# Second dense stage of a two-block kernel: first projection in two blocks around the input products, output projection in quarters, mixed rows by halves, one gate row spread last

## The reference

```python
mod = c_act @ w_ada[l] + b_ada[l]
sh1, sc1, g1, sh2, sc2, g2 = jnp.split(mod, 6, axis=-1)
h = _modulate(_rmsnorm(x, norm1_g[l]), sh1, sc1)
q, k, v, u = jnp.split(h @ w_in[l], [D_ATTN, 2 * D_ATTN, 3 * D_ATTN], axis=-1)
...
attn_out = _diff_attention(q, k, v, lam, lambda_init, subln_g[l])   # 4 heads, two softmaxes each
ssm_out = _s5(u, ...)              # diagonal state space, gelu z, then z * sigmoid(z @ w_glu + b_glu)
mix = jnp.concatenate([attn_out, ssm_out], axis=-1) @ w_out[l]
x = x + g1[:, None, :] * mix
h = _modulate(_rmsnorm(x, norm2_g[l]), sh2, sc2)
x = x + g2[:, None, :] * _moe(h, ...)       # 32 experts, top 4, w1 1024x2048, w2 1024x1024
```

## Time and profile before

| | |
|---|---|
| median of 3 runs | 1909.75 us (1908.7 to 1909.96) |
| profiled execution: its time, its span | 1911.13 us, 1909.1 us |
| PE busy | 1616.4 us (85%) |
| DVE busy | 470.0 us (25%) |
| ACT busy | 249.8 us (13%) |
| mean DMA rate over the span | 358 GB/s |
| dense stage two | 778.9 to 952.0 us of the span |
| mixture two | 952.0 to 1900 us of the span |

### The profile page before, as it was taken

One profiled execution on the slowest core, in us unless ns is written; L12 is line 12 of the kernel. 1 busy time (PEld: TensorE's weight loads), 2 busy tenths in 40 slices (PEclk: granted clock), 3 DMA queues, 4 the chain that ended last, 5 costly groups with the idle time before them and its releaser, 6 DMA issues. The chain is left out here.

```text
span 1909.1 us, 23699 instructions
## 1 busy us (share of the span) xinstructions
PE 1616.4 (85%) x9872; PEld 783.0 (41%) x9872; DVE 470.0 (25%) x749; ACT 249.8 (13%) x451; POOL 116.0 (6%) x267
## 2 busy tenths in 40 slices
PE   6999998676766667797799898989989989899896
PEld 6665545333323334464543333333333333333332
DVE  2632313110101100597421121221221212212123
ACT  2123322000000001114210000000000000000001
POOL 0030000793000000000000000000000000000000
PEclk9999998888778888897799999999999999999998
DMA  9556875999999999613568999999999999999994
GB/s 327 211 177 252 270 264 200 426 426 428 428 428 428 428 428 424 220 76 146 229 290 355 428 428 426 428 427 428 428 428 428 427 428 427 427 427 428 428 428 196
DMA packets 90270, 683.75 MB, mean 358 GB/s; under 512 B 18103, under 2 KB 21352, under 8 KB 53352
## 3 DMA queue, kind: packets, MB, share of 16 engines
q1 hardware_dynamic: 86466, 678.72, 86.3%
q10 hardware_dynamic: 3750, 4.26, 0.7%
HBM read 681.91 MB, written 1.05 MB: 358 GB/s over the span
## 5 line engine op out<-in xcount | busy, mean ns | idle before, releaser
L1391 PE MATMUL ps<-ring,hT 128*64 128x512 f32 x2048 | 464.4, 611 | 38.9 <-DMA ring<-in_w_dram 38.8
L1391 PEld LDWEIGHTS ps<-ring,hT 128*64 128x64 f32 x2048 | 158.1, 141 | 342.3 <-issue 341.4
L1386 PE MATMUL ps<-ring,hT 128*32 128x256 f32 x2048 | 161.6, 481 | 95.5 <-DMA ring<-in_w_up_dram 60.9
L1434 PE MATMUL ps<-ring,Wp 128*64 128x512 f32 x992 | 224.7, 612 | 14.3 <-ACT Wp L1476 14.3
L1386 PEld LDWEIGHTS ps<-ring,hT 128*32 128x32 f32 x2048 | 81.8, 133 | 176.4 <-issue 122.8
L1434 PEld LDWEIGHTS ps<-ring,Wp 128*64 128x64 f32 x992 | 71.7, 141 | 157.6 <-issue 139.7
L1525 DVE TENSOR_SCALAR Wp<-ps 128x1024 f32<-128x1024 f32 x16 | 19.6, 1225 | 430.0 <-PE ps L1391 430.0
L967 PE MATMUL ps<-ring,hT 128*128 128x512 f32 (+1 forms) x288 | 120.8, 573 | 0.0
L1469 ACT ACTIVATE mod<-Wp 128x1024 f32<-128x1024 f32 x16 | 17.0, 1061 | 782.5 <-DVE Wp L1525 782.5
L1430 PE MATMUL ps<-ring,m_hidT 128*32 128x512 f32 x480 | 69.2, 729 | 31.5 <-DMA ring<-in_w_down_dram 31.5
L1541 DVE TENSOR_TENSOR hT<-ps,Wp 128x512 f32<-128x512 f32 x32 | 20.6, 686 | 240.3 <-PE ps L1434 240.3
(11 more groups left out here) (453 smaller groups left out, 1435.2 us busy)
## 6 DMA issues: line engine op xcount, KB each, us to landing
ring<-in_w_dram SPq DMA_DIRECT2D x190, 2048.0 KB, 15.6
ring<-in_w_gate_dram SPq DMA_DIRECT2D x32, 2048.0 KB, 19.0
ring<-in_w_up_dram SPq DMA_DIRECT2D x32, 2048.0 KB, 20.1
ring<-in_w_down_dram SPq DMA_DIRECT2D x30, 2048.0 KB, 20.2
ring<-in_w_in_dram SPq DMA_DIRECT2D x14, 2048.0 KB, 15.6
ring<-in_w_ada_dram SPq DMA_DIRECT2D x12, 2048.0 KB, 11.4
ring<-in_w_out_dram SPq DMA_DIRECT2D x4, 2048.0 KB, 16.7
Wp<-in_w_down_dram SPq DMA_DIRECT2D x2, 2048.0 KB, 11.1
```

Of the source, the lines that this page charges most:

```text
L1386: ins = nt.matmul(ps[r:r + 32, u // 2, c:c + 256], xgT[:, t, x:x + 32], w[:, 512 * t:512 * t + 512].rearrange("q (p b s) -> q b p s", b=2, ...
L1391: ins = nt.matmul(ps[64 * e:64 * e + 64, b, :], xgT[:, 2 * u + t, 64 * e:64 * e + 64], w[:, c:c + 512], start=False, stop=u == 3 and t == ...
L1434: ins = nt.matmul(ps[r, C0 + h, :], hidT[:, 4 * u + t, r], w[:, c:c + 512], start=u == 0 and t == 0, stop=4 * u + t == FT - 1, tile_positi ...
```

## The change

`P0` keeps its first block in bank 6 and puts the second in bank 5; ACT copies each block as it is done, and `I0` is issued from inside the second block, before its fourth product. `Out` and `L` go by quarters (tile i, half h): `L0` to `L3`, of which the last two now stand behind `Glu`, and the state space half in four quarters, each with its own signal. DVE gates `ssT` in two halves, adds the mixed rows by halves, and starts the norm of tile 0 before the last half is added. ACT squares by halves, loads the sigmoid table early and the square root table ahead of its copies. `D` moves behind `H3`, `G2` ahead of `S1`. The g2 row is spread after the logits instead of between the output products.

```diff
@@ ORDER2 and the SP queue
-        ORDER2 = "P0 I0 R0 P1 I1 P2 C0 R1 P3 I2 G0 J0 P4 C1 R2 G1 H0 P5 S0 P6 C2 S1 I3 Y X0 X1 G2 E0 P7 T0 O0 E1 T1 O1 J1 J2 " \
-                 "U3 H1 H2 N M K L0 V3 C3 D G3 J3 H3 L1 Glu Out"
+        ORDER2 = "P0 R0 P1 I1 P2 C0 R1 P3 I2 G0 J0 P4 C1 R2 G1 H0 P5 S0 P6 C2 G2 S1 I3 Y X0 X1 E0 P7 T0 O0 E1 T1 O1 J1 J2 " \
+                 "U3 H1 H2 N M K L0 V3 C3 G3 J3 H3 D L1 Glu L2 L3 Out"
...
-                        sp.wait_ge(g_m, 1)
+                        sp.wait_ge(g_o, 1)
                         sp.dma_start(area[:, 1, :], moe2_src(0, AT + 1)).then_inc(aside2[1], 16)
@@ PE, P
+                                if n == 0 and cb == 1 and t == 3:
+                                    pe.wait_ge(p_ak, 1)
+                                    I(0)
-                                ins = nt.matmul(ps[:, 6 + n % 2, cb * 256:cb * 256 + 256], w[:, t, c:c + 128], hT[:, t, :],
+                                ins = nt.matmul(ps[:, 5, 0:256] if n == 0 and cb else ps[:, 6 + n % 2, cb * 256:cb * 256 + 256], w[:, t, c:c + 128], hT[:, t, :],
+                            if n == 0 and cb == 0:
+                                ins.then_inc(p_a, 1)
@@ ACT, P and Attn
+                    if n == 0:
+                        a.wait_ge(p_a, 1)
+                        na.activation(uT[:, 0], ps[:, 6, 0:256], ACT.Copy).then_inc(p_ak, 1)
+                        a.wait_ge(s2_proj, 1)
+                        na.activation(uT[:, 1], ps[:, 5, 0:256], ACT.Copy).then_inc(s2_pev, 1)
+                        return
...
+                    na.activation(lam[:, 6:7], K("eps"), ACT.Sigmoid)
@@ PE, mix
+                def mix(i, k, src, h):
+                    for c in range(4):
+                        if k and c % 2 == 0 and i == 0 and h == 0:
+                            pe.wait_ge(g_m, c // 2 + 1)
@@ PE, Out
-                    pe.wait_ge(g_m, 1)
-                    mix(0, 1, ssT).then_inc(g_o, 1)
+                    for i in range(NT):
+                        for h in range(2):
+                            mix(i, 1, ssT, h).then_inc(g_o, 1)
+                    pe.wait_ge(g_o, 4)
+                    pe.sem_inc(units_used, 3)
                     pe.wait_ge(k_ad, 4)
-                    spread_mod_pe(pe, 1, 1, k_sp, SPREAD)
-                    mix(1, 1, ssT).then_inc(g_o, 1)
-                    pe.wait_ge(g_o, 2)
-                    pe.sem_inc(units_used, 3)
                     for i in range(NT):
                         n3.pe_tile(pe, i, N3_BANKS)
                         n3.pe_logits(pe, i, q2_in, 160, q2_lg, wr2, brow2, 32, N3_LOGITS)
+                    spread_mod_pe(pe, 1, 1, k_sp, SPREAD)
@@ ACT, Out
+                    n3.act_ready()
                     spread_mod_act(a, (mod2[:, 0:2 * D],), 0, k_sp, k_ad, SPREAD)
+                    junk2 = wf[:, 3072:4096]
+                    n3.act_squares(a, 0, (0, 2), 1, junk2)
+                    n3.act_squares(a, 0, (1, 2), 2, junk2)
+                    n3.act_squares(a, 1, (0, 2), 3, junk2)
+                    n3.act_hT_half(a, 0, 0, N3_BANKS)
+                    n3.act_squares(a, 1, (1, 2), 4, junk2)
+                    n3.act_hT_half(a, 0, 1, N3_BANKS)
+                    n3.act_hT(a, 1, N3_BANKS)
                     spread_mod_act(a, (mod2[:, 2 * D:3 * D],), 1, k_sp, k_ad, SPREAD)
-                    n3.act_ready()
-                    for i in range(NT):
-                        n3.act_squares(a, i, (0, 1), i + 1, wf[:, 3072:4096])
-                        n3.act_hT(a, i, N3_BANKS)
@@ DVE, Out
+                    def add_mixed(i, h):
+                        c = slice(512 * h, 512 * h + 512)
+                        v.wait_ge(g_o, 2 * i + h + 1)
+                        link(nv.tensor_tensor(grow[:, c], ps[:, MIX[i][h], :], mod[:, D + 512 * h:D + 512 * h + 512], ALU.mult))
+                        nv.tensor_tensor(X[:, i, c], X[:, i, c], grow[:, c], ALU.add).then_inc(n3.sum, 1)
+                    for h in range(2):
+                        add_mixed(0, h)
+                    add_mixed(1, 0)
+                    v.wait_ge(k_ad, 4)
+                    n3.dve_root(v, link, 0)
+                    n3.dve_half(v, link, 0, 0)
+                    add_mixed(1, 1)
+                    n3.dve_half(v, link, 0, 1)
+                    n3.dve_tile(v, link, 1)
```

More of the change, by code:

```diff
@@ L329, in dve_tile, with dve_root, dve_half @@
             def dve_tile(self, v, link, i):
+                self.dve_root(v, link, i)
+                for b in range(2):
+                    self.dve_half(v, link, i, b)
+            def dve_root(self, v, link, i):
                 v.wait_ge(self.rt, i + 1)
                 link(nc.vector.reciprocal(st[:, 4 + i:5 + i], st[:, 2 + i:3 + i]))
+            def dve_half(self, v, link, i, b):
                 o = hn[:, i].rearrange("q t p -> q p t")
@@ L335, in dve_tile @@
                 g = self.gain.rearrange("q (p t) -> q p t", t=KC)
-                for b in range(2):
+                if True:
                     t = slice(4 * b, 4 * b + 4)
@@ L364, in act_squares, with act_hT_half @@
                     a.wait_ge(self.sd, self.squares)
+            def act_hT_half(self, a, i, b, banks):
+                a.wait_ge(self.tr, 2 * i + b + 1)
+                nc.scalar.activation(hT[:, 4 * b:4 * b + 4, i * 128:i * 128 + 128],
+                                     ps[:, banks[i][b], :].rearrange("p (t q) -> p t q", t=4), ACT.Copy).then_inc(self.ev, 1)
             def act_hT(self, a, i, banks):
                 for b in range(2):
-                    a.wait_ge(self.tr, 2 * i + b + 1)
-                    nc.scalar.activation(hT[:, 4 * b:4 * b + 4, i * 128:i * 128 + 128],
-                                         ps[:, banks[i][b], :].rearrange("p (t q) -> p t q", t=4), ACT.Copy).then_inc(self.ev, 1)
+                    self.act_hT_half(a, i, b, banks)
             def pe_tile(self, pe, i, banks):
@@ L1956, in bass_block_pair @@
                            "a2_variance", "a2_root", "a2_normed", "a2_outT", "a2_outT_kept"))
-        e_h, e_bu, e_u, e_pr, e_y, e_y1, e_sg, e_z = (S(n) for n in (
-            "ssm_input_half", "ssm_input", "ssm_input_rotated", "ssm_products", "ssm_out", "ssm_gelu_arg", "ssm_gelu_sig", "ssm_gelu"))
+        p_a, p_ak, e_h, e_bu, e_u, e_pr, e_y, e_y1, e_sg, e_z = (S(n) for n in (
+            "proj2_first_block", "proj2_first_block_kept", "ssm_input_half", "ssm_input", "ssm_input_rotated", "ssm_products", "ssm_out", "ssm_gelu_arg", "ssm_gelu_sig", "ssm_gelu"))
         k_sp, k_ad = S("mod2_spread"), S("mod2_kept")
@@ L2021, in I @@
                 def I(q):
-                    pe.wait_ge(s2_pev, 1 if q < 2 else 2)
                     if q:
+                        pe.wait_ge(s2_pev, 1 if q < 2 else 2)
                         pe.wait_ge(e_u, q)
@@ L2090, in Attn @@
                     ins.then_inc(d_nt, 1)
-                def mix(i, k, src):
-                    for h in range(2):
-                        for c in range(4):
-                            ins = nt.matmul(ps[:, MIX[i][h], :], src[:, c, i * 128:i * 128 + 128], unit(K_OUT2 + 2 * k)[:, c, h * 512:h * 512 + 512],
-                                            start=k == 0 and c == 0, stop=k == 1 and c == 3)
+                def mix(i, k, src, h):
+                    for c in range(4):
+                        if k and c % 2 == 0 and i == 0 and h == 0:
+                            pe.wait_ge(g_m, c // 2 + 1)
+                        ins = nt.matmul(ps[:, MIX[i][h], :], src[:, c, i * 128:i * 128 + 128], unit(K_OUT2 + 2 * k)[:, c, h * 512:h * 512 + 512],
+                                        start=k == 0 and c == 0, stop=k == 1 and c == 3)
                     return ins
@@ L2102, in Gate, with MixA @@
                     spread_mod_pe(pe, 0, 1, g_ad, (2, 3, 4, 5))
-                def MixA(i):
+                def MixA(n):
                     pe.wait_ge(g_adk, 4)
@@ L2107, in MixA @@
                     unit_arrived(pe, K_OUT2)
-                    mix(i, 0, aT)
+                    mix(n // 2, 0, aT, n % 2)
                 def Glu():
@@ L2363, in Out @@
                 def Out():
-                    v.wait_ge(g_s, 4)
-                    nv.tensor_tensor(ssT, ssT, zT, ALU.mult).then_inc(g_m, 1)
+                    for h in range(2):
+                        c = slice(2 * h, 2 * h + 2)
+                        v.wait_ge(g_s, 2 * h + 2)
+                        nv.tensor_tensor(ssT[:, c], ssT[:, c], zT[:, c], ALU.mult).then_inc(g_m, 1)
                     v.wait_ge(g_adk, 4)
-                    for i in range(NT):
-                        v.wait_ge(g_o, i + 1)
-                        mixed = ps[:, MIX[i][0]:MIX[i][0] + 2, :].rearrange("p b c -> p (b c)")
-                        t = grow[:]
-                        link(nv.tensor_tensor(t, mixed, mod[:, D:2 * D], ALU.mult))
-                        nv.tensor_tensor(X[:, i, :], X[:, i, :], t, ALU.add).then_inc(n3.sum, 1)
-                        v.wait_ge(k_ad, 4)
```

(6 more changed lines are left out.)

## The result

The changed kernel took 1904.07 us (median of 8 runs, 1899.27 to 1905.96), the kernel before 1909.08 beside it (8 runs, 1904.76 to 1911.22): a ratio of 0.9976, 95% interval 0.9965 to 0.9988, that is 2.3 to 6.7 us less. 1905.0 was forecast. The same kernel timed again on another occasion gave 1901.63 against 1908.34, ratio 0.9967 (0.9954 to 0.998).

A forecast was written before the change was run, and what follows sets the result against it. The end was taken to follow when PE gets through its first expert pair. Terms 1.0 + 0.6 + 1.65 + 1.75 − 0.2 = 4.8 us took the profiled 1911.13 to 1906.3, the median to 1905.0; range 1902.6 to 1908.2.

The forecast's parts named there:

- What bounds the end: Mixture two: the program's end follows PE getting through its first expert pair; stage two's gain carries one for one.
- Rival 3: Mixture two: stage two's gain is lost there, the change does nothing, 1909 to 1909.8 us; chance 0.10.
- Head: Start of stage two: DVE starts 2.9 us earlier, PE only 0.6; gain carried on 0.8, bounds nothing and 2.9.
- Rival 2: Head of stage two: DVE's whole head start carries, 2.1 us more won, 1902.9 us; chance 0.06.
- Output product and `C3`: First output quarter to last products: Glu 7.1 us earlier, mostly given back; gain so far 1.0, head included.
- Last products: Stage two's last output products: 0.6 us from the spread moved away, 1.65 from the clock staying up.
- Rival 1: Last products: the clock falls again since the spread lowers it; gain 3.15, time 1906.6 us; chance 0.14.
- Mixed rows and norm: DVE's mixed rows and norm by halves: tile 1's norm ends at 939.1, adding 1.75 us.
- End: Behind the norm: logits and choice keep their distance, choice at 946.4; the g2 spread behind the logits costs 0.2 us.
- Logits and choice keep their distance to the norm: End of stage two: logits and choice of experts follow the norm as before, choice moving from 951.41 to 946.4.
- Rival 5: A clock rising later before the experts, or a quarter more waiting in ACT's order: 1 us less gained, 1906; chance 0.10.
- Rival 4: Between C3 and the last quarter: the clock stays down, gain gone after 9.6 us, slower from 17 us; chance 0.04.

The follow-up runs named there:

- e9: The changed kernel again, same code, timed and profiled once more: 1901.63 us against 1908.34, ratio 0.9967.
- e1: The kernel before with only the head changed (P0 in two blocks, I0 inside the second): ratio 0.9995.
- e6: The changed kernel with the ten router loads (D) back ahead of quarter 3's gelu and without the early sigmoid table load: ratio 0.9991.
- e4: The changed kernel with mixed rows, squares and norm by whole tiles as before, PE's quarters kept: ratio 0.9972.
- e5: The kernel before with only the g2 spread moved behind the logits: ratio 0.9989.
- e3: The changed kernel with L2 and L3 ahead of Glu instead of behind it: ratio 0.9981.
- e2: The changed kernel with the g2 spread back between the products of tile 0 and tile 1: ratio 0.9984.
- e7: The changed kernel with nine products nobody reads in PE's waits at the end of the stage, three behind the last spread: ratio 0.9953.
- e12: The changed kernel with unread products mid-stage and at its end, three behind the last spread, L1 ahead of C3: 1897.42 us against 1908.10, ratio 0.9939.
- e11: The changed kernel with only five unread products, between the halves of tile 0's transposes: ratio 0.9965.
- e8: The changed kernel with unread products mid-stage and at its end, one behind the last spread, L1 ahead of C3: 1897.44 us against 1906.29, ratio 0.9953.
- e10: The changed kernel with unread products at the stage's end, one instead of three behind the last spread: ratio 0.9969.

## Why the prediction was right, point by point

**What bounds the end.** Right. The first expert product came 6.67 us earlier, and the last up products of the stream ended 6.8 earlier (1865.09 against 1871.90). Rival 3, the gain lost in mixture two, is out: the gap before the stream moved from 1009.3 to 1002.7. But one sign that the prediction named as speaking against it did come: the span became only 5.3 shorter, not 6.67. The difference is the last pair's down products, partly at half clock here, which e9 does not have.

**Head.** The mechanism was right, the size 1.4 to 1.5 instead of 0.8. `P1` ends 1.0 earlier, not 0.6. Of this, the change is about 0.75: PE's pause of 0.69 is gone whole, so that "less the handling of the switch" was a cost that did not come. The other 0.24 is the clock, which rose 12.5 us into the stage and not 13.0; e1, where it rose at 12.9, saved 0.79. From there to `C2` another 0.38 is won, in e1 too, since neither `C0` nor `C2` waits for DVE any longer; 0.18 was forecast. Rival 2 is out.

**Output product and `C3`.** `Glu` 8.05 us earlier, nearly all given back: as forecast (7.1 and 0.2 left). That `D` had to go behind `H3` for this was costed at nothing with its cover named; e6, which takes it and the early table load back, prices the two at 1.7 us once `L1` is a quarter. The term is right as a sum, but it is not one edit: without these two moves 1.7 us of the other gains would be gone. Two things in it came otherwise. The first quarter took 6.07 us and not 5.5, as the clock rose 4.8 us behind its start, and the wait of 0.4 ahead of `C3` did not show (it did where the clock rose sooner, 0.6 us in e4). And the step from `L0` to the last products moves with the clock by as much as was won: 27.16 before and 26.89 after, but 26.81 in e5, which has the old program there.

**Last products.** 0.6 and 1.65 were forecast, 2.52 measured. e3 shows that the fall comes back with the pause, e5 that it does not need the second spread, and e2 that this spread costs 0.85 between the products, which is the 0.6 that was too small, and brings no fall there. The fall before was read 0.3 too late: shares of 0.57 and 0.72 in windows of 1 us put it at 918.1 and the rise at 921.6, 3.4 us at half clock, and half of that, 1.7, is what the 1.65 stood for. Whether the pause would do it without the spread behind it was not tried. Rival 1 is out for this order of the work. But one row that I leaned on bears nothing: that the clock stayed at 1.00 behind the pause of `S1`. Behind the same pause (2.12 us) it fell to 0.50 in the changed kernel and stayed there until 866, and 79.8 to 83.2 us into the stage it fell in each of the twelve other executions too. It costs nothing there, since PE is not last: from `C2` to `L0` lie 35.9 us with that fall and without. The rows are of the changed kernel:

```profile
859.00:860.00 1.00, 1.00 (x8) 0.83 (x8) 1.00 (x1) 1.00 (x1) 0.00 (x0) 0.70 0.00 0
860.00:861.00 1.00, 0.94 (x6) 0.39 (x4) 0.97 (x2) 0.07 (x1) 0.00 (x0) 0.50 0.00 0
```

**Mixed rows and norm.** 1.75 forecast, 2.03 measured; e4 gives 2.1.

**End.** The term "Logits and choice keep their distance to the norm" failed. The distance grew from 4.99 to 5.59 (6.00 in e9): the clock had fallen earlier relative to the work, in tile 0's logits and not behind them, and tile 1's transposes stood behind slow logits of tile 0. In e3, where it fell later, the distance is 4.99. The spread itself, which I charged with 0.2, cost nothing: ACT's last copy ended at 945.57, DVE's choice at 945.54. Rival 5 named a clock that rises later ahead of the experts; here it rose 1.7 us sooner behind the barrier (0.80 gained), in e9 0.9 later (0.4 lost). It works in both directions.

**Rival 4**, slower through the clock, did not happen in any of the kernels with `C3` between two quarters.

The errors of the steps, 0.6 and 0.1 and 0.3 and 0.3 too little, 0.4 too much, the two clock effects of 0.8 and 1.4 behind the barrier and 0.3 of an earlier start of the stage nearly cancel: 5.3 us of span for 4.8. That the median hit within 1 us owes something to luck. One execution of the same program differs from the next by about a microsecond at each fall of the clock, and the second timing of the changed kernel, 1901.63, lies below the lower end of the forecast's range, 1902.6.

## What to carry to other kernels

When two engines take turns at being last, a head start of one is worth only what the other saves: find the next wait of the engine that is freed. Moving work under a pause can pay twice, where the pause goes with a fall of the clock, and cutting a long step that hid something else makes that something visible. Where changes are worth a tenth of a per cent, compare steps in the trace from a common start, several executions of each, and let times only bound the sum.

## What the runs showed of the hardware

The granted clock makes equal programs differ. With the same code ahead of it, the first rotation came 17.3 to 17.4 us into the stage where the clock had risen from 1.2 to 2.4 GHz by 9.8 us (e4, e7, e12), and 18.3 to 18.9 where it rose at 11.6 to 12.9 (the nine others with the new head). In the last pair of experts the down products take 1.65 us more in four of fourteen executions. A pause of 2.1 us behind `S1` was met by a fall in thirteen of fourteen executions, not in the kernel before; a pause of 1.02 us with one-row products behind it was followed by one in four of four.

The same narrow logits (16 instructions of 32 columns) take 1.93 us at full clock and 3.46 to 3.6 at half, and a gather of 32 instructions 3.84 and up to 6.47, so a fall in a stretch that waits mostly for DVE still costs microseconds. Products that nobody reads, put into PE's waits, moved the fall from 155 to 156 us of the stage (the changed kernel and e9) to none (e7), to 162.8 (e11), 162.2 (e8) and 166.5 (e10), but not reliably: in e12, with as many of them at the end as e7, it fell at 159.9, in the middle of the last three.
